# Seven block products in place of eight in four of eleven weight slots of the down projections

## What is computed

```python
def swiglu_ffn(h, w13, w2):
    gate, up = jnp.split(h @ w13, 2, axis=-1)
    return (jax.nn.silu(gate) * up) @ w2
...
x = x + 0.5 * swiglu_ffn(rms_norm(x, ffn1_norm[l]), ffn1_w13[l], ffn1_w2[l])
```

## Time and profile before

| | us |
|---|---|
| median of 3 runs (1209.71 to 1213.11) | 1212.18 |
| the profiled execution | 1209.79 |
| its span, first to last instruction | 1208.1 |
| TensorE busy | 1191.5 |
| VectorE busy | 786.5 |
| ScalarE busy | 610.5 |
| GpSimd busy | 80.1 |

### The profile page before, as it was taken

One profiled execution on the slowest core, in us unless ns is written; L12 is line 12 of the kernel. 1 busy time (PEld: TensorE's weight loads), 2 busy tenths in 40 slices (PEclk: granted clock), 3 DMA queues, 4 the chain that ended last, 5 costly groups with the idle time before them and its releaser, 6 DMA issues.

```text
span 1208.1 us, 16080 instructions
## 1 busy us (share of the span) xinstructions
PE 1191.5 (99%) x6352; PEld 1011.9 (84%) x6352; DVE 786.5 (65%) x941; ACT 610.5 (51%) x770; POOL 80.1 (7%) x151
## 2 busy tenths in 40 slices
PE   8999999999999999999999999999999999999998
PEld 6888888988888888899898888888888888888886
DVE  4766547997665654788877756553688666565545
ACT  5544426565544443565644544543556755445333
POOL 1000003001000000400002000000114000000000
PEclk9999999999999999999999999999999999999999
DMA  8987764552588775545203688686355347877630
GB/s 272 318 279 250 236 217 147 160 192 59 177 271 244 243 243 175 193 157 174 88 1 105 193 274 256 218 255 211 136 206 202 131 129 233 259 257 230 227 136 36
DMA packets 174547, 235.32 MB, mean 195 GB/s; under 512 B 13993, under 2 KB 131849, under 8 KB 174473
## 3 DMA queue, kind: packets, MB, share of 16 engines
q1 hardware_dynamic: 174472, 234.30, 60.0%
HBM read 221.67 MB, written 12.58 MB: 194 GB/s over the span
## 4 chain that ended last, share of the span: by engine, by line
PE 93%; DVE 4%; ACT 1%; POOL 1%; DMA 0%; issue 0%; SPq 0%; DVEq 0%; ACTq 0%
PE bank L1717 28%; PE bank L1718 28%; PE bank L1719 28%; PE bank L1751 1%; PE bank L2146 1%; PE bank L2163 1%; PE bank L2171 1%; DMA raw<-in_ffn_w_dram 0%; PE bank L1970 0%; DVE xs L1523 0%; DVE bv L1378 0%; PE bank L2268 0%; DVE xs L1127 0%; PE bank L2290 0%; PE bank L1957 0%
## 5 line engine op out<-in xcount | busy, mean ns | idle before, releaser
L1112 DVE TENSOR_TENSOR wlo<-raw,whi 128x2048 fp32r<-128x2048 f32 (+1 forms) x190 | 415.9, 2194 | 236.4 <-ACT whi L457 236.4
L457 ACT ACTIVATE whi<-raw 128x2048 fp32r<-128x2048 f32 x190 | 362.9, 1914 | 227.2 <-PE bank L1719 218.4
L1717 PE MATMUL bank<-whi,xThi 128*128 128x512 f32 x1024 | 401.8, 392 | 0.9 <-DVE xTlo L1659 0.8
L1719 PE MATMUL bank<-whi,xTlo 128*128 128x512 f32 x1024 | 398.9, 390 | 0.0
L1718 PE MATMUL bank<-wlo,xThi 128*128 128x512 f32 x1024 | 398.5, 389 | 0.0
L1717 PEld LDWEIGHTS bank<-whi,xThi 128*128 128x128 f32 x1024 | 192.3, 188 | 41.4 <-DVE xTlo L1659 1.4
L1719 PEld LDWEIGHTS bank<-whi,xTlo 128*128 128x128 f32 x1024 | 192.2, 188 | 40.3
L1718 PEld LDWEIGHTS bank<-wlo,xThi 128*128 128x128 f32 x1024 | 192.3, 188 | 38.8
L1717 PE MATMUL bank<-whi,hThi 128*128 128x512 f32 x352 | 137.3, 390 | 0.0
L1719 PE MATMUL bank<-whi,hTlo 128*128 128x512 f32 x352 | 137.0, 389 | 0.0
L1718 PE MATMUL bank<-wlo,hThi 128*128 128x512 f32 x352 | 136.9, 389 | 0.0
(11 more groups left out here) (425 smaller groups left out, 1064.3 us busy)
## 6 DMA issues: line engine op xcount, KB each, us to landing
raw<-in_ffn_w_dram SPq DMA_DIRECT2D x176, 256.0 KB, 4.5
raw<-in_ffn_w_in_dram SPq DMA_DIRECT2D x176, 256.0 KB, 4.0
raw<-in_ffn_w_dram SPq DMA_DIRECT2D x22, 1024.0 KB, 5.3
raw<-in_ffn_w_out_dram SPq DMA_DIRECT2D x22, 1024.0 KB, 5.4
raw<-in_gdn_w_in_dram SPq DMA_DIRECT2D x16, 1024.0 KB, 5.5
hidden<-hblk SPq DMA_DIRECT2D x44, 256.0 KB, 5.1
hraw<-hidden SPq DMA_DIRECT2D x176, 64.0 KB, 3.3
raw<-in_ple_w_gate_dram SPq DMA_DIRECT2D x8, 1024.0 KB, 5.0
```

The costliest lines, as they stand in the source:

```text
L457: act.activation(whi[w % SPLIT][:], raw[w % RAW][:], ACT.Copy).then_inc(w_hi, 1)
L1112: dve.tensor_tensor(wlo[w % SPLIT][:, c], raw[w % RAW][:, c], whi[w % SPLIT][:, c].bitcast(F32), ALU.subtract).then_inc(w_lo, 1)
L1717: pe.matmul(psum, lhs[0], rhs[0], start=start, stop=False, skip_group_check=True)
L1719: return pe.matmul(psum, lhs[1], rhs[0], start=False, stop=stop, skip_group_check=True)
```

## The change

In each down projection the weight pairs 2, 3, 5 and 6 of 0 to 10 get the Winograd form of Strassen's scheme: a 2 x 2 by 2 x 2 block product by seven block products. The four weight blocks of such a pair (128 x 512 each) are two channel blocks by two output halves; the four activation blocks (128 x 128 each) are two token tiles by two channel blocks.

- Each such pair is followed by an empty slot: no load, but VectorE writes four blocks of weight sums into the raw buffer of that slot (`combine`: one 128x1024 and two 128x512 subtractions, with a wait after the first and the second). A down projection has 15 slots. In the slot of the pair itself only three of four blocks (1536 columns) are split; the slot of the sums is split whole.
- GpSimd forms four activation sums for each pair (`hidden_sums`: one 128x512 addition of high and low part, then four 128x128 ones) into `h_sum`, which has two places; from the third pair on it waits until the low part of the sums two pairs earlier is made. ScalarE and VectorE split the sums (`sums_hi`, `sums_lo`) into the place of the x operand, which is idle in the down projection. The first two are split at the start of the down stage, the other two behind the split of hidden block 9 and ahead of the split of the seventh slot.
- TensorE (`seven`) does 3 products in the slot of the pair and 4 in that of the sums, into banks 4, 7, 6, 5, 1, 0 and 3. Banks 6, 7 and 3 are those of the outputs; what is in 4, 0, 5 and 1 belongs to several output quarters.
- When the last seven-product slot is used, and after the split of the last weight slot, VectorE adds the shared banks into X (`shared_sums`: 4 + 3 + 2 + 2 additions of 128x512, with a wait after each group). The ordinary four additions follow.

```diff
+    SEVEN = (2, 3, 5, 6)
+    def stream_down(name, w):
...
+            slots.append([(("rows", 2), v[:, 2 * s:2 * s + 2, :])])
+            if s in SEVEN:
+                slots.append([])
...
# ScalarE, split and ffn
+                    if w in COMBINED:
+                        act.wait_ge(sem("seven_w"), COMBINED.index(w) + 1)
...
+                    c = slice(512 if w in SEVEN_SLOTS else 0, SLOT)
+                    act.activation(whi[w % SPLIT][:, c], raw[w % RAW][:, c], ACT.Copy).then_inc(w_hi, 1)
...
+                def sums_hi(m):
+                    act.wait_ge(sem("seven_sum"), len(SEVEN) * f + m + 1)
+                    act.activation(sum_hi[:, m], h_sum[:, m % 2], ACT.Copy).then_inc(sem("seven_hi"), 1)
+                act.wait_ge(w_used, first[f"down{f}"])
+                sums_hi(0)
+                sums_hi(1)
                 split(first[f"down{f}"] + SPLIT + 2)
                 hidden_hi(NBLK - 2)
+                for m in range(2, len(SEVEN)):
+                    sums_hi(m)
                 split(first[f"down{f}"] + SPLIT + 4)
                 hidden_hi(NBLK - 1)
...
# GpSimd, between the norms
+            def hidden_sums(f):
+                for m, s in enumerate(SEVEN):
+                    n = len(SEVEN) * f + m
+                    pool.wait_ge(sem("ffn_lo"), NBLK * f + s + 1)
+                    if n:
+                        pool.wait_ge(sem("seven_sum"), n)
+                    step(pool.tensor_tensor(h_all[:], hThi[:, s].bitcast(F32), hTlo[:, s].bitcast(F32), ALU.add))
+                    if n >= 2:
+                        pool.wait_ge(sem("seven_lo"), n - 1)
+                    v = h_sum[:, m % 2]
+                    pool.tensor_tensor(v[:, S3], h_all[:, 2], h_all[:, 0], ALU.subtract)
+                    step(pool.tensor_tensor(v[:, S1], h_all[:, 2], h_all[:, 3], ALU.add))
+                    step(pool.tensor_tensor(v[:, S2], v[:, S1], h_all[:, 0], ALU.subtract))
+                    pool.tensor_tensor(v[:, S4], h_all[:, 1], v[:, S2], ALU.subtract).then_inc(sem("seven_sum"), 1)
...
# VectorE, called by split(n) ahead of the wait for the high part
+            def combine(w):
+                dve.wait_ge(raw_in[w % RAW], arrived[w])
+                dve.wait_ge(w_lo, split_done(w + 1 - RAW))
+                b = raw[w % RAW][:].rearrange("p (q c) -> p q c", q=4)
+                t = raw[(w + 1) % RAW][:].rearrange("p (q c) -> p q c", q=4)
+                step(dve.tensor_tensor(t[:, 0:2], b[:, 0:1].broadcast_to([P, 2, 512]), b[:, 1:3], ALU.subtract))
+                step(dve.tensor_tensor(t[:, 2], b[:, 2], t[:, 0], ALU.subtract))
+                dve.tensor_tensor(t[:, 3], b[:, 3], t[:, 2], ALU.subtract).then_inc(sem("seven_w"), 1)
...
# VectorE, in residual after the split of the last slot
+            def shared_sums(done, scale):
+                def into(product, *quarters):
+                    for t, h in quarters:
+                        c = slice(h * 512, (h + 1) * 512)
+                        ins = dve.scalar_tensor_tensor(out=X[:, t, c], in0=product[:], scalar=scale, in1=X[:, t, c],
+                                                       op0=ALU.mult, op1=ALU.add)
+                    step(ins)
+                dve.wait_ge(w_used, done)
+                into(bank[4], (0, 1), (0, 0), (1, 1), (1, 0))
+                into(bank[0], (0, 0), (1, 1), (1, 0))
+                into(bank[5], (0, 0), (1, 0))
+                into(bank[1], (1, 1), (1, 0))
...
# TensorE, in place of rows() for these slots
+                product(bank[4], hidden(0, 0), ring(w), 1, begins)
+                product(bank[7], hidden(0, 1), ring(w), 3, False)
+                pe.wait_ge(sem("seven_lo"), len(SEVEN) * f + m + 1)
+                product(bank[6], combined(S4), ring(w), 2, False).then_inc(w_used, 1)
+                pe.wait_ge(w_lo, split_done(w + 1))
+                product(bank[5], combined(S1), ring(w + 1), 0, begins)
+                product(bank[1], combined(S3), ring(w + 1), 1, begins)
+                product(bank[0], combined(S2), ring(w + 1), 2, begins)
+                product(bank[3], hidden(1, 1), ring(w + 1), 3, False).then_inc(w_used, 1)
```

More of the change, by code:

```diff
@@ L82, in stream_wide @@
             slots.append([(("rows", 2), v[:, 2 * s:2 * s + 2, :])])
+    SEVEN = (2, 3, 5, 6)
+    def stream_down(name, w):
+        first[name] = len(slots)
+        v = w.rearrange("(k p) n -> p k n", p=P)
+        for s in range(KF // 2):
+            slots.append([(("rows", 2), v[:, 2 * s:2 * s + 2, :])])
+            if s in SEVEN:
+                slots.append([])
     stream_gate_up("up0", a["ffn1_w13"][0])
-    stream_wide("down0", a["ffn1_w2"][0])
+    stream_down("down0", a["ffn1_w2"][0])
     stream_pairs("mix", a["w_in"][0])
@@ L90, in build_program @@
     stream_gate_up("up1", a["ffn2_w13"][0])
-    stream_wide("down1", a["ffn2_w2"][0])
+    stream_down("down1", a["ffn2_w2"][0])
     stream_blocks("gdn", a["gdn_w_in_2"][0], (6, 0, 1, 2, 3, 4, 5, 7))
@@ L94, in build_program @@
     stream_gate_up("up2", a["ffn_w_in_2"][0], 0)
-    stream_wide("down2", a["ffn_w_out_2"][0])
+    stream_down("down2", a["ffn_w_out_2"][0])
     stream_wide("ple_g0", a["ple_w_gate_2"][0])
@@ L101, in build_program @@
     stream_gate_up("up3", a["ffn_w_in_2"][1], 1)
-    stream_wide("down3", a["ffn_w_out_2"][1])
+    stream_down("down3", a["ffn_w_out_2"][1])
     stream_wide("ple_g1", a["ple_w_gate_2"][1])
@@ L110, in build_program @@
     WIDE = ["down0", "mix_out", "down1", "gdn_out", "down2", "ple_g0", "sb_out", "down3", "ple_g1"]
-    wide_slots = {n: (KF if n[:4] == "down" else KD) // 2 for n in WIDE}
+    wide_slots = {n: KF // 2 + len(SEVEN) if n[:4] == "down" else KD // 2 for n in WIDE}
+    pair_at = {s + sum(x < s for x in SEVEN): s for s in range(KF // 2)}
+    seven_at = {s + sum(x < s for x in SEVEN): m for m, s in enumerate(SEVEN)}
+    SEVEN_SLOTS = [first[f"down{f}"] + i for f in range(4) for i in sorted(seven_at)]
+    COMBINED = [w + 1 for w in SEVEN_SLOTS]
     NORM = [a["ffn1_norm"][0], a["mix_norm"][0], a["ffn2_norm"][0], a["final_norm"], a["ln_mix_2"][0],
@@ L208, in build_program @@
             gate_s = lent.enter_context(nc.sbuf_tensor("gate_s", [P, NT, D], F32))
-        hThi, hTlo, hnat, hblk, hraw, p_in, pThi, pTlo, pp, row_tap, row_tap4 = region(
+        hThi, hTlo, hnat, hblk, hraw, h_all, h_sum, p_in, pThi, pTlo, pp, row_tap, row_tap4 = region(
             [("hThi", [P, NBLK, 4, P], F32R), ("hTlo", [P, NBLK, 4, P], F32R),
-             ("hnat", [P, 2, NT, 256], F32), ("hblk", [P, 2, 4, P], F32), ("hraw", [P, 2, 4, P], F32)],
+             ("hnat", [P, 2, NT, 256], F32), ("hblk", [P, 2, 4, P], F32), ("hraw", [P, 2, 4, P], F32),
+             ("h_all", [P, 4, P], F32), ("h_sum", [P, 2, 4, P], F32)],
             [("p_in", [P, NT, PLE], F32), ("pThi", [P, 2, SEQ], F32R), ("pTlo", [P, 2, SEQ], F32R),
@@ L214, in build_program @@
             [("row_tap", [P, P], F32), ("row_tap4", [W4 * QKV, P], F32)])
+        S1, S2, S3, S4 = range(4)
+        sum_hi, sum_lo = (x[:].rearrange("p (m a) (b c) -> p m (a b) c", a=2, c=P) for x in (xThi, xTlo))
         hdram = [nc.dram_tensor(f"hidden{i}", [P, 4, P], F32, kind="Internal").ap() for i in range(2)]
@@ L1079, in mixer3 @@
                             root(krs[:, i, t, h], kms[:, i, t, h], kss[:, i, t, h], P, ("s_kss", "s_krs"), 4 * i + 2 * b + t + 1)
+            def hidden_sums(f):
[12 more added lines that the diff above has]
+                    pool.tensor_tensor(v[:, S4], h_all[:, 1], v[:, S2], ALU.subtract).then_inc(sem("seven_sum"), 1)
             norm(0)
+            hidden_sums(0)
             mixer1()
             norm(2)
+            hidden_sums(1)
             mixer2()
             norm(5)
+            hidden_sums(2)
             norm(6)
@@ L1088, in _ @@
             norm(9)
+            hidden_sums(3)
             norm(10)
@@ L1105, in split @@
                     w = split_to[0]
+                    if w in SEVEN_SLOTS:
+                        combine(w)
                     dve.wait_ge(w_hi, split_done(w))
@@ L1110, in split @@
                                           ALU.subtract).then_inc(w_half, 1)
-                    c = slice(SLOT // 2 if w in HALVED else 0, SLOT)
+                    c = slice(SLOT // 2 if w in HALVED else 512 if w in SEVEN_SLOTS else 0, SLOT)
                     dve.tensor_tensor(wlo[w % SPLIT][:, c], raw[w % RAW][:, c], whi[w % SPLIT][:, c].bitcast(F32),
@@ L1161, in residual @@
                 split(last_group(name) + SPLIT)
-                return add
+                if name[:4] == "down":
+                    shared_sums(last_group(name), scale)
+                return add
+            def shared_sums(done, scale):
[10 more added lines that the diff above has]
+                into(bank[1], (1, 1), (1, 0))
             def ffn(f):
@@ L1200, in ffn, with sums_lo @@
                         setup()
+                def sums_lo(m):
+                    dve.wait_ge(sem("seven_hi"), len(SEVEN) * f + m + 1)
```

(30 more changed lines are left out.)

1 line of the change is left out of this document (removed).

## The result

The changed kernel takes 1224.7 us (median of 4 runs, 1222.6 to 1225.2) against 1211.8 before (1209.7 to 1213.1): ratio 1.0105, 95% interval 1.0086 to 1.0124. That is 13 us slower, where 18.4 were forecast. The profiled execution spans 1223.1 us, 15.0 more than before; the profiled execution before was at the low end of its kernel's range, so of the 15.0 us in the rows the medians show 13. (The 1212.2 of the table before the change is the median of three executions; with a fourth it is 1211.8.)

A forecast was written before the change was run, and what follows sets the result against it. TensorE, busy 1191.5 of 1208.1 us, was taken as the bound. Stages 11.3 us longer (the -10.9 of saved matmuls included) plus 7.1 at their ends gave +18.4 on 1212.2: 1230.6 us, range 1206 to 1238, the forecast's own 1222 to 1238.

The forecast's parts named there:

- The wait before slot 6: Down stages: GpSimd's late sum 3 holds up ScalarE and VectorE's split of slot 6; TensorE 3.8 us late.
- lo 6: VectorE's half of the weight split of slot 6; forecast to end 24.2 us after a down stage's first matmul.
- rival C: Down stages: lock holds, but GpSimd gets in after one VectorE op; +9 us, 1221; chance 0.12.
- One sign: Down stages: no idle left on VectorE between its weight splits of slots 5 and 10.
- The collision: Down stages: VectorE instructions with two SBUF inputs and GpSimd ones reading SBUF exclude each other for the whole instruction.
- Slots 9 and 10: Each down stage: VectorE's splits for these slots come 1.2 and 0.5 us late for TensorE.
- L: Start of a down stage's last four slots; forecast 40.9 us after the stage's first matmul (T), 38.1 before.
- Rival D: Down stages: the waits also slow the clock; one slot a stage at 1.2 GHz is +22 us; chance 0.04.
- The end: Ends of the four down stages: late last load and 11 adds cost 1.4 + 3.6 + 1.1 + 1.1 = 7.1 us.
- the first term: Four down stages, each 2.8 us longer up to the last four slots: 11.3 us, saved matmuls already included.
- A: Down stages: GpSimd's sums are in time, slipping in or costing VectorE nothing; -0.9 us, 1211.3; chance 0.17.
- B: Down stages: VectorE keeps up altogether and loads land early; -9.7 us, 1202.5; chance 0.17.

The follow-up runs named there:

- the best version: Kernel with four places for the sums and 3 of 11 shared adds behind the first ordinary one, pairs 1, 3, 5, 6: 1201.4 us, ratio 0.993.
- the run with memsets: Changed kernel with GpSimd's activation sums replaced by memsets of the same tiles, which read nothing: 1210.0 us, ratio 0.9996.
- the run with four places: Changed kernel with four places for the activation sums in place of two, so GpSimd makes all in the up projection: 1209.0 us, ratio 0.999.

## Why the prediction was right, and where its sizes were off

**The saving and what binds.** 48 matmuls at 0.2267 us, 10.9 us, was right: the best version gets 2.72 us in a stage.

**The wait before slot 6.** Place, cause and order of events were as forecast: GpSimd's sum 3, ScalarE behind it, hi and lo of slot 6 behind that. Forecast lo 6 at T+24.2 and 3.8 us late, measured T+22.9 and 2.6. The term that was mis-sized is GpSimd's turn: I let it starve through lo 5, hTlo and the sum split, but it gets in after each VectorE op. Its two ops from 146.82 to 150.08 ended behind one VectorE op each. So rival C's mechanism is the true one in this point, at T+18.1 for sum 3 where the forecast took 19.35 and C 17. A small GpSimd op alone is 0.46 us, my 0.4 was low. One sign was wrong by my own schedule: VectorE does idle between lo 5 and lo 10, 1.56 us for sum 3 and 1.11 for hi 6.

**The collision.** The forecast leaned on the earlier trace rows and was right in kind: the run with memsets points to the reads, the one with four places shows what the lateness costs (15.7 us, where 13 to 15 were expected). Off was the price to VectorE, which the forecast set at the whole GpSimd op: a small one adds 0.14 to 0.29 us to a VectorE one (1.51 for 1.22, 0.83 for 0.69), seven ops of down0 some 1.5 us together. GpSimd pays more: 1.45 and 2.40 us for 0.46.

**Slots 9 and 10.** Forecast 1.2 and 0.5 us late in each stage. Measured from start to start: 0.95 and 0.46 in down1 and down3, nothing in down0 and down2, where the slow clock took the time instead. L = T+39.8, not T+40.9: 6.8 us for four where I had 11.3, and lo 6 being 1.3 us earlier than forecast is the reason.

**Rival D.** Its stretches at half clock did come, in two stages, but they added nothing: L is T+39.8 with them and without. TensorE had only to keep up with VectorE there. Its premise was misread: 0.8 us is the longest wait in the earlier trace rows, not in the trace before, which has one of 2.2 at its start and one of 1.3 at 8.25.

**The end.** Forecast 1.4, 3.6, 1.1, 1.1: 7.1 us. Measured 1.6, 2.6, 2.0, 1.6: 7.8. The shared adds took 7.05 us (forecast 7.2), and lo 14 ended at L+7.6 in down0 (forecast 6.9). Both halves of the argument were needed: without the adds the ends cost nothing, and with lo 14 on time (pairs 1, 3, 4, 5) all 11 adds cost 1.0, near the lower bound of 1.2. The load of slot 14 was not moved by itself.

**Luck.** 6.8 + 7.8 = 14.6 us of the 18.4: the first term was 4.5 too large, the second 0.7 too small. The median, 1224.7, lies nearer to C's 1221 than to 1230.6, and the difference of the medians is 2 us less than that of the profiled spans. It is inside the forecast's range, 1222 to 1238, because that range begins 1 us above C.

**Rivals A and B.** Not this kernel. But A is what the run with four places is (1209.0; I had worked out 1211.3), so A's price was good and only its condition was missing; the best version beats B's 1202.5 by a us.

## What to carry to other kernels

Before giving idle GpSimd work with SBUF reads, look at what VectorE does at that time: here both were late together, and whoever waits for GpSimd in an in-order queue passes the delay to all behind it. Make such sums a stage earlier, for the price of two more places. And when TensorE work is traded for VectorE work, spread it: here four pairs gave 1215.6 us with three in a row and 1201.4 with at most two, while the number of products is equal.

## What the hardware showed that was not expected

- A TensorE gap of 2.4 us was followed by some 3 us at a granted clock of 0.50 in two of four stages of the changed kernel, and in all four of the run without the shared adds. Shorter waits can be followed by it too: in the profile of the best version TensorE waited 0.81 and 0.79 us for `xs` behind down1 (490.75 and 492.19), and from 492.9 to 496.2 the clock was 0.50. The kernel before has the same two waits, 0.62 and 0.79, without such a stretch. What decides is open.
- A slow stretch need not cost anything: where VectorE feeds TensorE late anyway, L stayed at T+39.8. In the run with pairs (1, 3, 4, 5), down3 had one (from 1154.2) and its L is T+39.6, against T+38.6 in the other three.
- GpSimd's tensor_tensor gets its turn after one VectorE op, also when the next is queued without a gap. In the kernel before, a 128x1 op waited through two; the difference is not explained.
